# A three-layer block on one core: queries and keys of the linear attention in 512-wide products of both token halves, and the middle of the last projection in 512 weight columns

## What is computed

```python
def _gla(h, w_in, w_gate, gate_bias, out_g, w_out):
    q, k, v, g, lr = jnp.split(h @ w_in, ...)      # 1024, 1024, 2048, 2048 and 16 columns
    log_alpha = jax.nn.log_sigmoid(lr @ w_gate + gate_bias) / 16
    cum = cumsum of log_alpha within chunks of 64 tokens; total = cum[-1]
    kc = k * exp(total - cum)
    state = exp(total) * state + k_i^T v_i;  o = q_i @ state      # over the chunks
    return (_rmsnorm(o, out_g) * jax.nn.silu(g)) @ w_out
x = x + _gla(_rmsnorm(x, norm_g), ...)
```

## Time and profile before

| | |
|---|---|
| median of 3 runs | 1630.15 us |
| profiled execution | 1632.96 us, its span 1631.1 us |
| TensorE busy | 1587.4 us (97%), 13421 products |
| DVE busy | 975.3 us (60%) |
| ACT busy | 792.6 us (49%) |
| DMA | 253.2 MB, mean 155 GB/s |
| mean granted clock | 0.994 |

### The profile page before, as it was taken

The page is one execution under the profiler, slowest core; times in us unless marked ns, Lnnn a source line. Parts: engine busy times, 40 slices in busy tenths (PEclk is TensorE's granted clock), DMA queues, the critical chain, the costliest instruction groups (busy, mean ns, idle before and its releaser), DMA issues. The chain is left out here.

```text
span 1631.1 us, 30898 instructions
## 1 busy us (share of the span) xinstructions
PE 1587.4 (97%) x13421; PEld 1489.2 (91%) x13421; DVE 975.3 (60%) x1314; ACT 792.6 (49%) x1138; POOL 93.7 (6%) x83
## 2 busy tenths in 40 slices
PE   8999999999999999989999999999999999999999
PEld 7989998899988999989999899999999988877899
DVE  6686647756455654476555678887556764444543
ACT  6643236432235654454443487776446424454532
POOL 2120003100000000031000000000100000000000
PEclk9999999999999999989999999999999999999999
DMA  9543222422373237547666444445544645555462
GB/s 297 188 130 104 92 92 89 152 98 92 116 229 105 98 115 259 169 99 222 196 189 183 151 132 140 156 139 160 195 167 141 203 149 181 193 170 179 140 209 91
DMA packets 77247, 253.23 MB, mean 155 GB/s; under 512 B 8817, under 2 KB 17042, under 8 KB 76472
## 3 DMA queue, kind: packets, MB, share of 16 engines
q1 hardware_dynamic: 76456, 251.04, 47.8%
q0 software_dynamic: 656, 0.21, 0.1%
HBM read 248.53 MB, written 2.69 MB: 154 GB/s over the span
## 5 line engine op out<-in xcount | busy, mean ns | idle before, releaser
L307 DVE TENSOR_TENSOR w_lo<-w_raw,w_hi 128x1024 fp32r<-128x1024 f32 (+1 forms) x452 | 551.0, 1223 | 501.6 <-ACT w_hi L302 501.2
L302 ACT ACTIVATE w_hi<-w_raw 128x1024 fp32r<-128x1024 f32 (+1 forms) x452 | 470.5, 1045 | 573.5 <-PE ps L360 418.3
L358 PE MATMUL ps<-xt,w_hi 128*128 128x256 f32 x1968 | 580.1, 295 | 12.0 <-DVE w_lo L307 8.5
L359 PE MATMUL ps<-xt,w_hi 128*128 128x256 f32 x1968 | 560.4, 285 | 0.0
L360 PE MATMUL ps<-xt,w_lo 128*128 128x256 f32 x1968 | 560.3, 285 | 0.0
L358 PEld LDWEIGHTS ps<-xt,w_hi 128*128 128x128 f32 x1968 | 380.9, 194 | 31.2 <-issue 19.2
L359 PEld LDWEIGHTS ps<-xt,w_hi 128*128 128x128 f32 x1968 | 381.4, 194 | 1.4 <-issue 1.0
L360 PEld LDWEIGHTS ps<-xt,w_lo 128*128 128x128 f32 x1968 | 380.8, 193 | 0.0
L358 PE MATMUL ps<-proj_rounded,w_hi 128*128 128x256 f32 x512 | 144.3, 282 | 1.2 <-PEq L2227 0.6
L360 PE MATMUL ps<-proj_rounded,w_lo 128*128 128x256 f32 x512 | 144.7, 283 | 0.0
L359 PE MATMUL ps<-proj_rounded,w_hi 128*128 128x256 f32 x512 | 144.3, 282 | 0.0
(11 more groups left out here) (408 smaller groups left out, 2041.4 us busy)
## 6 DMA issues: line engine op xcount, KB each, us to landing
w_raw<-in_a_w_in SPq DMA_DIRECT2D x128, 512.0 KB, 3.6
w_raw<-in_w_in SPq DMA_DIRECT2D x120, 512.0 KB, 3.5
w_raw<-in_b_w_in SPq DMA_DIRECT2D x96, 512.0 KB, 3.5
w_raw<-in_w_out SPq DMA_DIRECT2D x32, 512.0 KB, 4.2
w_raw<-in_a_w_out SPq DMA_DIRECT2D x32, 512.0 KB, 3.6
w_raw<-in_b_w_out SPq DMA_DIRECT2D x32, 512.0 KB, 3.8
arena<-in_cmp_w SPq DMA_DIRECT2D x3, 1024.0 KB, 6.3
arena<-in_x SPq DMA_DIRECT2D x4, 512.0 KB, 6.4
```

Of the source, the lines that this page charges most:

```text
L302: k.nc.scalar.activation(k.wh[:, p % RING, 0:m], k.raw[:, p % RAW, 0:m], ACT.Copy).then_inc(k.hi_made, 1)
L307: k.nc.vector.tensor_tensor(k.wl[:, p % RING, 0:m], k.raw[:, p % RAW, 0:m], k.wh[:, p % RING, 0:m].bitcast(F32), ALU.subtract).then_inc(k. ...
L358: pe.matmul(os, h[:, cs], xh, start=st and ct == 0, stop=False, skip_group_check=True)
L359: pe.matmul(os, h[:, cs], xl, start=False, stop=False, skip_group_check=True)
```

## The change

`third_plan` gives the eight chunks of queries and keys the kind "W" in place of "T". `last_plan` replaces the six "tok" chunks in the middle by three "V" chunks of 512 columns; the first and the last chunk stay. The plan then has five chunks, so `turns` is (1, 2, 3).

```diff
 def third_plan():
-    return (one_tile("T", 6160 - P) + tiles("W", 0, 8) + [("V", (4096 + GLA_DV * j,), GLA_DV) for j in range(GLA_H)]
+    return (one_tile("T", 6160 - P) + [("W", (CW * j,), CW) for j in range(8)] + [("V", (4096 + GLA_DV * j,), GLA_DV) for j in range(GLA_H)]
             + [("V", (2048 + GLA_DV * j,), GLA_DV) for j in range(GLA_H)])

 def last_plan():
-    return [("tok", (0,), CW)] + toks(CW, 6) + [("tok", (7 * CW,), CW)]
+    return [("tok", (0,), CW)] + [("V", (CW + 2 * CW * j,), 2 * CW) for j in range(3)] + [("tok", (7 * CW,), CW)]
```

## The result

The changed kernel takes 1639.98 us (median of 4, 1639.22 to 1641.84) against 1630.34 of before measured beside it: ratio 1.0054, 95% interval 1.0042 to 1.0066, so 6.8 to 10.8 us slower. The ratio is not the quotient of the two medians: they lie 9.6 us apart, and 1.0054 is 8.8 us. The forecast was +4.7 us, 1634.9, with a range up to 1639.3. With the ratio on the 1630.15 of the forecast it is 1639.0, inside the range by 0.3 us; the median itself lies 0.7 us above it. The direction and both mechanisms held, the size was about half of what came.

The account below looks back on a forecast made before the run. TensorE, busy 97% of the span, was taken to bound the kernel, with DVE setting the pace over the queries. Queries and keys +2.1 us and last projection +2.6 us gave +4.7 us on 1630.15, so 1634.9 us, range 1631.3 to 1639.3.

Parts of the forecast that it names:

- both mechanisms: TensorE waits on DVE's reductions over the queries, and waits after the turns in the last projection for late copies and read-outs.
- Part 1: Queries and keys: 3.8 us longer over the queries, 1.7 us saved by the other 16 pieces, +2.1 us in sum.
- W: Queries and keys: DVE's time to read out one tile, a reduction and a product with rsb, put at 1.05 us.
- 2 us of waiting before piece 14: Queries: TensorE was to idle about 2 us before this piece, released by DVE's reduction, as a sign of being right.
- The saving of the keys: Pieces outside the delayed query stretch: 16 pieces save 0.107 us each, 1.7 us, with DVE's read-outs hidden over the keys.
- Part 2, waits: Last projection: some 1.8 us at each of three turns, +5.4 us, and once 0.3 us in chunk 1's second half.
- Part 2, saving: Last projection: 24 "V" pieces at 2.72 us against 2.85 save 0.13 us each, 3.1 us for 288 products.
- hidden waits: Rival: the queries' waits are covered and only the turns cost, sum -0.8 us, 1629.4 us; chance 0.12.
- the faster ones: Rival: the "V" read-out doesn't hold TensorE and the queries' waits are hidden too, -6.5 us, 1623.7 us; chance 0.03.
- "W" k-tile went at 0.320: Rival: "W" products stream at 0.320 us a k-tile, 16 pieces save 3.4 us more, 1631.5 us; chance 0.08.
- The clock fell: Rival: the clock falls in the new waits, one to three times at the turns, +1.7 to +5.1 us, about 1638.5; chance 0.13.
- The rival without a fixed cost: Rival: no fixed cost per product, so no saving in either stretch, +3.8 and +5.7 us, 1639.6 us; chance 0.02.

Follow-up runs that it names:

- e1: Kernel before with only the queries and keys made kind "W", last projection unchanged: 1634.55 us, ratio 1.0017 to before.
- e4: Kernel before with only the keys (chunks 5 to 8) made kind "W", the queries staying "T": 1630.83 us, ratio 0.9993 to before.
- e7: As e1, without the product with rsb after each tile's reduction, so queries and keys stay unscaled: 1633.65 us, ratio 1.0015 to before.
- e3: As e2, with the turns one chunk earlier, (0, 1, 2) in place of (1, 2, 3): 1631.50 us, ratio 0.9999 to before.
- e2: Kernel before with only the last projection changed to "V" chunks, turns after chunks 1, 2 and 3: 1637.22 us, ratio 1.0036 to before.
- e11: The whole change with turns 0 and 1 after chunk 0, turn 2 after chunk 1, turn 3 after chunk 2: 1634.78 us, ratio 1.0020 to before.

## Why the prediction was right or wrong

- **Part 1 was right in mechanism and nearly in size.** Forecast +2.1, in the profiles +2.8 (and +3.3 in e1). From the norm's sums, pieces 11, 12, 14 and 18 were forecast to start 24.44, 31.11, 38.74 and 50.59 us later; they started 24.55, 31.22, 38.84 and 50.71 us later. W, taken from a reduction of the same size elsewhere, was 1.06 for 1.05. The wait for chunk 0's bank (0.45 us, at piece 6) was missed; DVE set the pace there, so it cost nothing further on. One sign came out otherwise: 2 us of waiting before piece 14 were forecast, 0.24 came, with the piece starting when forecast. The granted clock had fallen, and pieces 12 and 13 took 7.4 us between them instead of the 5.55 of two pieces at full clock; the fall used up 1.8 us of the wait.
- **The saving of the keys came short.** A k-tile of "W" was put at 0.3467. The changed kernel has just that from 1271 to 1312, but 0.353 before it (1243 to 1255) and 0.3533 after the mixer's first scores; e4, e1 and e7 have 0.353 over all of the keys. The saving of 16 pieces is 0.8 (e4), not 1.7. In the changed kernel that is about half of the 0.7 us by which part 1 was too low: up to the mixer's first scores 3.2 us were lost for a forecast of 2.9, the rest came behind them.
- **Part 2, waits: right.** Forecast 1.8 us for each turn and 0.3 once; the profile has 1.8 and 0.3, with the releasers named, and in e3 the three are gone and 5.2 us with them.
- **Part 2, saving: the step that failed.** "A piece of V costs 12 x 0.2267 = 2.72" took a price that was measured with tokens from `xt` and used it for tokens from `proj_rounded`. There it is 2.81 against 2.85 for "tok": 24 pieces save 1.0 us, not 3.1. That is 2.1 of the 2.3 us by which part 2 was too low (+2.6 forecast, +4.9 measured). The text gave this term no bounds, while it gave them to "W", because it thought the shape had been seen. With them (nothing saved at the worst) part 2 would have reached +5.7.
- **The rivals.** The hidden waits and the faster ones fell with e1 and e2, and no "W" k-tile went at 0.320. The clock fell once, in the queries, right behind the wait of 3.62 us (row below, at 0.57 over 4 us, as in the earlier trace rows), and cost nothing there: piece 14 still started when DVE let it. The same fall stands in e1, e7 and e11, the others with "W" over the queries, and in no profile without it. At the turns it did not fall. The rival without a fixed cost, put at 1639.6 with a chance of 0.02, is the nearest of all to the measured 1640.0, but its mechanism is not what came: the keys alone save 0.8 us (e4), and the "V" pieces 1.0. That its time comes out is in part luck. Still, it was dismissed too fast: the 0.0133 us per removed product, on which the forecast went, holds for "V" with `xt` standing and for "W" at its quicker level; at 0.3533 a k-tile a removed product is worth 0.0067, and with `proj_rounded` standing 0.0034. The Trainium skill's 2.5 ns (TensorE: Matmul & The Clock Gate, "Back-to-back issue gap") is near the last and far from the first. But the distances themselves are not those of its formula: an estimate from it gives 109.2 and 215.8 ns for 256 and 512 columns, where `proj_rounded` has 118.8 and 234.2. That the difference comes near doesn't confirm the rule.

```profile
1263.00:1267.00 4.00, 3.81 (x13) 3.29 (x14) 3.90 (x11) 0.00 (x0) 0.00 (x0) 0.57 0.54 195
```

- **The sum.** +4.7 forecast, +7.7 in the profiles, +8.8 by the ratio with 6.8 to 10.8 as the interval, +9.6 between the medians. What the last two have over the profiles isn't explained by a part; it lies within the interval and within the 4 us by which the unchanged start of the kernel varies from profile to profile.

## What to carry to other kernels

Before a unit of work is made larger, look for what is scheduled by its number: the turns kept their place by chunk, and since a chunk now reached two blocks of x, each came one chunk too late. Splitting a read-out in two halves the time that a producer may run ahead with two banks, so the price is not only the second operation (e7 took it away, and the 3.6 us before piece 12 stayed) but all that the consumer has queued ahead of the first. And a duration that is taken from the trace belongs to its operands too, not only to its shape; give it bounds when only the shape was seen.

## What the runs showed of the hardware

The distance between products of one shape takes several levels at a full granted clock. For 512 columns it is 0.2267 us with the tokens from `xt` standing and 0.2342 with those from `proj_rounded`; for 256 columns it is the other way round, 0.120 and, in the mean, 0.1188. With the high parts from `proj_rounded` and the low ones from `xt` all three 512-wide products of a group went at 0.230. In the "W" stretches the same code ran at 0.3467 or 0.3533 us a k-tile in one execution, and changed level only where TensorE's stream was interrupted; in e7, at piece 18, by under 0.1 us and with no wait listed. In the last projection of e1 the 256-wide products went at 0.120 between two turns, at 0.1173 between the next two and at 0.1187 after that. None of the runs says what sets the level.
